# Two-block decoder: the second block's last four feed-forward groups go down in pairs, and feed-forward loops are written out

## The chip, the core and the metric

The kernel runs on one core of one Trainium2 chip. The metric is the device time of one execution in microseconds (us). On this core TensorE multiplies, ScalarE (ACT) and VectorE (DVE) prepare operands and do the elementwise work, GpSimd (POOL) does little here, and SyncE (SP) issues nearly all of the weight transfers. The engines run on their own and wait for each other through semaphores.

## What is computed

256 tokens of width 1024 go through two blocks of two layers each. The change touches the feed-forward parts. In the second block that is:

```python
def _swiglu(x, w_gate, w_up, w_down):
    h = jax.nn.silu(jnp.einsum('bsd,df->bsf', x, w_gate)) * jnp.einsum('bsd,df->bsf', x, w_up)
    return jnp.einsum('bsf,fd->bsd', h, w_down)
...
    for l in range(DEPTH):
        mix = _hybrid_mixer(x, rel_bias, w_in[l], b_in[l], w_attn_proj[l], w_ret_proj[l], w_out[l])
        x = _layer_norm(ALPHA * x + mix, ln1_g[l], ln1_b[l])
        ffn = _swiglu(x, w_ffn_gate[l], w_ffn_up[l], w_ffn_down[l])
        x = _layer_norm(ALPHA * x + ffn, ln2_g[l], ln2_b[l])
```

Here the hidden width is 2816 and all values are float32. The first block's feed-forward has a hidden width of 4096, a squared ReLU in place of the gated SiLU, and 512 hidden columns at a time.

## The kernel before

**Float32 products out of three passes.** A weight is split into a rounded part and the rest, `hi` and `lo`, and so is an activation. A product is hi x hi, plus hi x lo of the activation, plus lo of the weight x hi. The weights come in *units* of up to 4 x 128 rows by 512 columns (1 MB). Each unit is brought by SP into one of four slots (`raw`), copied by ACT into `whi` (function `hi`, L1157) and subtracted by DVE into `wlo` (function `lo`, L1600). `whi` and `wlo` have two places each, so ACT may split unit c once TensorE has used unit c - 2. SP may fill a slot once DVE has split the unit that was in it, four units back. TensorE's function `unit` (L639) waits for `hi`, does 4 matmuls for each block of 128 rows (two row tiles, two activation parts), waits for `lo` and does 2 more. A full unit is 24 matmuls of 128x512, a *half-size* unit of 2 x 128 rows is 12.

**The second block's feed-forward.** The hidden width is worked in FJ = 11 groups of 256 columns. A group needs two full units, gate and up side by side (`chunk`, 48 matmuls into PSUM pair 0). Then ACT applies SiLU and DVE multiplies (`inner2`), both on `H2`. TensorE turns the result round with 4 transposes (`inner_turn2`), ACT copies it into `MH` (`turn_hi`) and DVE subtracts into `ML` (`turn_lo`). The way down is two half-size units (`down2`, 24 matmuls into PSUM pairs 1 and 2). TensorE's order is software-pipelined: gate and up of group j + 1, down of group j, transposes of group j + 1. So the 24 matmuls of the way down cover SiLU and product. Groups 2 to 10 of gate and up are one loop, `Fori(0, FJ - 2)`, on TensorE, ACT and DVE, whose waits add 4 x i to a semaphore's value. SP's loop over the groups is already written out. The first block has a loop of 6 turns of the same kind.

**The end of a layer.** The last group's way down is done by `last_columns` (L683): the first row tile (m = 0) for both column halves, then the second (m = 1). After m = 0 `s_half` is raised, and DVE may start on the residual and the layer norm of row tile 0 (`residual`, `row_spread`, `row_norm`). Between the `hi` and the `lo` matmuls of the very last half, TensorE transposes the normalised row tile 0 for what follows (`turn_ahead`). After the last `lo` matmuls DVE does the second half of row tile 1 and its norm. In DVE's order the last group's work is followed by `lo_first` twice (the next layer's first two units, which have buffers of their own), and only then by the residual. ACT has `hi_first` twice at the same place. In the last layer there is no next layer, so these two are missing, but the transposes of row tile 0 are still made.

Of the kernel before, what the change touches and what calls it, by code (L numbers as in the profile page):

```python
# [31 lines left out]
P = 128  # L32
# [5 lines left out]
COLS = 512  # L38
UK = 4
UNIT = UK * COLS  # L40
RAW = 4
# [34 lines left out]


U_OUT, U_MLP, U_PLE0, U_DN7, U_PLE1, UNITS1 = 14, 18, 48, 49, 51, 56
V_RET, V_GATE, V_AP, V_RP, V_OUT, V_FFN, UNITS2 = 14, 30, 46, 48, 56, 60, 104
# [39 lines left out]
FIRSTS = (0, U_MLP, U_PLE1 + 1), (0, V_FFN)  # L119

# [74 lines left out]
def program(nc, a, out):  # L195
# [3 lines left out]
    with ExitStack() as ctx:  # L199
# [123 lines left out]
        s_raw = [Tally(sem(f"s_raw{n}"), (UNITS1 // RAW, UNITS2 // RAW + more), step=16)  # L323
                 for n, more in enumerate((1, 1, FJ - 1, FJ - 1))]
# [99 lines left out]
        def _(sp):  # L424
# [74 lines left out]
            for L in range(DEPTH):  # L499
# [54 lines left out]
                for k in range(2):  # L554
                    gate_up(0, V_FFN + k, k, (V_FFN + k) % RAW)
                for i in range(FJ - 1):
                    for k in range(2):
                        gate_up(i + 1, 4 * i + V_FFN + 2 + k, k, (V_FFN + 2 + k) % RAW)
                    for n in range(2):
                        src = down[bass.ds(L, 1)][:, bass.ds(i * 256, 256), n * COLS:(n + 1) * COLS].rearrange(  # L560
                            "l (k p) n -> p (l k) n", p=P)
                        unit(1, L, 4 * i + V_FFN + 4 + n, src, 2, COLS, (V_FFN + 4 + n) % RAW)
                for n in range(2):
                    unit(1, L, V_FFN + 42 + n, rows(down, L, (FJ - 1) * 256, 2, n * COLS, COLS), 2, COLS,
                         (V_FFN + 42 + n) % RAW)
# [12 lines left out]
        def landed(blk, L, i, c):  # L578

            o, slot = i + c // RAW, c % RAW  # L580
            k = o + 1
            if blk and c >= V_FFN:
                if slot < 2:
                    k = o + 2
                elif c >= UNITS2 - 2:
                    k = o + FJ
                else:
                    k = o * 2 - (2 * (V_FFN // RAW) - 17)
            return s_raw[slot].at(blk, L, k)

        def size(blk, c):
# [7 lines left out]
            small_unit = c >= UNITS2 - 2 or (c >= V_FFN + 4 and c % RAW < 2)  # L599
            return 2 * COLS if small_unit else UNIT  # L600

# [36 lines left out]
        def _(pe):  # L638
# [220 lines left out]
            for L in range(DEPTH):  # L859
# [138 lines left out]
            for L in range(DEPTH):  # L998
# [132 lines left out]
                def inner_turn2(i, j):  # L1131
                    pe.wait_ge(s_h.sem, s_h.at(1, L, i + j + 1))
                    turn(1, L, i, T2_FFN + 2 * j, H2, 2, per=1)

                def down2(i, c, first, t):
                    pe.wait_ge(s_tfree.sem, s_tfree.at(1, L, 2 * i + t))
                    for n in range(2):
                        unit(1, L, i, c + n, MH, ML, 0, 2, COLS, bank_pair(1 + n), first, False)

                first_chunk(1, L, V_FFN, T2_FX, 1, 2)  # L1140
                second_chunk(1, L, V_FFN + 2, lambda: inner_turn2(0, 0))
                down2(0, V_FFN + 4, True, T2_FFN + 2)
                inner_turn2(0, 1)
# [9 lines left out]
        def _(act):  # L1153
# [100 lines left out]
            for L in range(DEPTH):  # L1254
# [104 lines left out]
                with act.Fori(0, 6) as i:  # L1359
# [45 lines left out]
            for L in range(DEPTH):  # L1405
# [57 lines left out]
                def inner2(i, j, used, bank=0):  # L1463

                    act.wait_ge(s_used.sem, s_used.at(1, L, 4 * i + used))
                    act_(H2, pair(bank)[:, :, 0:256], ACT.Silu).then_inc(s_act.sem, 1)

                hi(1, L, 0, V_FFN + 2)
                inner2(0, 0, V_FFN + 2, 2)
                hi(1, L, 0, V_FFN + 3)  # L1470
                turn_hi(1, L, 0, T2_FFN, 2, MH, per=1)
                with act.Fori(0, FJ - 2) as i:
                    his(1, L, i, V_FFN + 4, V_FFN + 5)
                    inner2(i, 1, V_FFN + 4)
                    his(1, L, i, V_FFN + 6, V_FFN + 7)
                    turn_hi(1, L, i, T2_FFN + 2, 2, MH, per=1)
                e = 4 * (FJ - 2)
                his(1, L, 0, V_FFN + 4 + e, V_FFN + 5 + e)
                inner2(0, FJ - 1, V_FFN + 4 + e)
                his(1, L, 0, V_FFN + 6 + e, V_FFN + 7 + e)  # L1480
                turn_hi(1, L, 0, T2_FFN + 2 * (FJ - 1), 2, MH, per=1)
# [115 lines left out]
        def _(dve):  # L1597
# [208 lines left out]
            for L in range(DEPTH):  # L1806
# [154 lines left out]
                with dve.Fori(0, 6) as i:  # L1961
# [44 lines left out]
            for L in range(DEPTH):  # L2006
# [186 lines left out]
                def inner2(i, j, bank=0):  # L2193
                    dve.wait_ge(s_act.sem, s_act.at(1, L, i + j + 1))
                    tt(H2, H2, pair(bank)[:, :, 256:512], ALU.mult).then_inc(s_h.sem, 1)

                lo(1, L, 0, V_FFN + 2)
                inner2(0, 0, 2)
                lo(1, L, 0, V_FFN + 3)
                turn_lo(1, L, 0, T2_FFN, 2, MH, ML, per=1)  # L2200
                with dve.Fori(0, FJ - 2) as i:
                    los(1, L, i, V_FFN + 4, V_FFN + 5)
                    inner2(i, 1)
# [41 lines left out]
```

## Time and profile before

| | |
|---|---|
| time, median of 3 runs | 1979.17 us (1978.88 to 1979.22) |
| the profiled execution: its own time | 1976.11 us |
| its span, first to last instruction | 1974.3 us |
| busy: PE, PEld, DVE, ACT, POOL | 96%, 79%, 60%, 45%, 4% |
| the chain that ended last | PE 85%, DVE 7%, ACT 3% |
| mean granted TensorE clock | 0.979 |
| read from HBM | 333 MB, 172 GB/s over the span |

PE is TensorE's matmuls, PEld its weight loads. A matmul's shown duration (about 0.39 us) overlaps the next one's, so the spacing of starts tells the pace. The granted clock has two levels, 1.00 (2.4 GHz) and 0.50 (1.2 GHz). The chain is followed back from the last instruction to what released each one. The second block's feed-forward parts lie at 1179 to 1376 us (layer 0) and at 1783 us to the end (layer 1), the first block's loops at about 215 to 350 us and 605 to 740 us.

### The profile page before, as it was taken

The numbers are of one execution on the slowest core, as the hardware profiler recorded it, in microseconds if no ns is written. First come the engines' busy times: TensorE is split into PE (matmuls) and PEld (weight loads), VectorE is DVE, ScalarE is ACT, GpSimd is POOL, SyncE is SP. The second block draws the span as 40 slices with busy tenths as digits, with TensorE's granted clock in tenths as the row PEclk, the third lists the DMA queues.
The fourth block names the chain that finished last, engine by engine and source line by source line (L and its number), as shares of the span: only waits on it lengthen the run. The fifth ranks groups of instructions, "written<-read, shape, count | busy, mean of one in ns | idle before, by whom it ended". The sixth has DMA issues, their size and how long they took to land.

```text
span 1974.3 us, 23117 instructions
## 1 busy us (share of the span) xinstructions
PE 1897.8 (96%) x9135; PEld 1562.0 (79%) x9135; DVE 1175.4 (60%) x1368; ACT 886.3 (45%) x1071; POOL 83.3 (4%) x100
## 2 busy tenths in 40 slices
PE   7988999999899999999999999998999999999997
PEld 5877888877778888888877778887888877778885
DVE  5775554657765547456566575446556566574555
ACT  5544444555454445344345434443344355444442
POOL 6300000021100000000000000000000000000000
PEclk9988999999799999999999999999999999999998
DMA  8423555544656555654455754557563455645552
GB/s 256 142 65 113 173 189 180 196 157 135 90 173 193 189 173 208 210 189 151 144 170 175 238 174 147 183 183 242 180 222 114 152 184 189 220 156 177 185 187 89
DMA packets 194385, 340.17 MB, mean 172 GB/s; under 512 B 9342, under 2 KB 59422, under 8 KB 194304
## 3 DMA queue, kind: packets, MB, share of 16 engines
q1 hardware_dynamic: 189072, 327.76, 49.8%
q0 software_dynamic: 5232, 11.29, 3.1%
q8 instruction: 55, 0.90, 0.2%
q14 instruction: 26, 0.21, 0.0%
HBM read 333.24 MB, written 5.77 MB: 172 GB/s over the span
## 4 chain that ended last, share of the span: by engine, by line
PE 85%; DVE 7%; ACT 3%; DVEq 2%; issue 2%; DMA 0%; SPq 0%; ACTq 0%
PE G L647 19%; PE G L648 18%; PE G L652 18%; PE T L700 5%; PE A L647 4%; PE A L648 4%; PE A L652 4%; PE G L662 2%; PE G L663 2%; PE G L668 2%; DVE wlo L1605 1%; PE T L749 1%; PE A L662 1%; ACT whi L1155 1%; PE A L759 1%
## 5 line engine op out<-in xcount | busy, mean ns | idle before, releaser
L1605 DVE TENSOR_TENSOR wlo<-raw,whi 128x2048 fp32r<-128x2048 f32 (+3 forms) x300 | 630.0, 2102 | 570.6 <-ACT whi L1155 570.4
L1155 ACT ACTIVATE whi<-raw 128x2048 fp32r<-128x2048 f32 (+3 forms) x300 | 527.1, 1759 | 588.1 <-PE G L652 513.1
L647 PE MATMUL G<-whi,XH 128*128 128x512 f32 (+1 forms) x1408 | 560.1, 398 | 7.6 <-DVE XL L1619 6.3
L648 PE MATMUL G<-whi,XL 128*128 128x512 f32 (+1 forms) x1408 | 549.5, 390 | 0.0
L652 PE MATMUL G<-wlo,XH 128*128 128x512 f32 (+1 forms) x1408 | 346.2, 388 | 0.0
L647 PEld LDWEIGHTS G<-whi,XH 128*128 128x128 f32 x1408 | 266.1, 189 | 64.3 <-DVE XL L1619 8.0
L648 PEld LDWEIGHTS G<-whi,XL 128*128 128x128 f32 x1408 | 266.2, 189 | 53.9 <-issue 1.9
L652 PEld LDWEIGHTS G<-wlo,XH 128*128 128x128 f32 x1408 | 263.9, 188 | 53.6
L700 PE MATMUL T<-ident,arena 128*128 128x128 f32 x804 | 118.6, 288 | 23.0 <-ACT arena L1155 17.3
L700 PEld LDWEIGHTS T<-ident,arena 128*128 128x128 f32 x804 | 97.8, 148 | 42.1 <-ACT arena L1155 17.9
L1155 ACT ACTIVATE arena<-T 128x512 f32<-128x512 f32 (+2 forms) x92 | 46.1, 550 | 159.2 <-PE T L700 159.2
L647 PE MATMUL G<-whi,MH 128*128 128x512 f32 x216 | 84.4, 391 | 0.0
L648 PE MATMUL G<-whi,ML 128*128 128x512 f32 x216 | 84.0, 389 | 0.0
L647 PE MATMUL A<-whi,MH 128*128 128x512 f32 x192 | 74.7, 389 | 0.0
L648 PE MATMUL A<-whi,ML 128*128 128x512 f32 x192 | 74.7, 389 | 0.0
L647 PE MATMUL A<-whi,XH 128*128 128x512 f32 (+1 forms) x160 | 61.3, 385 | 0.0
L648 PE MATMUL A<-whi,XL 128*128 128x512 f32 (+1 forms) x160 | 59.8, 375 | 0.0
L1155 ACT ACT_TABLE_LOAD x40 | 51.3, 1283 | 13.6 <-PE T L700 8.1
L2013 DVE TENSOR_TENSOR arena<-G,swap 128x1024 f32<-128x1024 f32 (+1 forms) x36 | 43.4, 1206 | 22.7 <-PE G L652 18.9
L652 PE MATMUL G<-wlo,MH 128*128 128x512 f32 x216 | 55.1, 389 | 0.0
L1155 ACT ACTIVATE arena<-G,nm 128x128 f32<-128x128 f32 (+1 forms) x80 | 32.5, 418 | 47.0 <-DVE nm L1671 47.0
L1155 ACT ACTIVATE MH<-T 128x256 fp32r<-128x256 f32 (+1 forms) x82 | 33.3, 456 | 41.1 <-PE T L700 41.1
(237 smaller groups left out, 2240.1 us busy)
## 6 DMA issues: line engine op xcount, KB each, us to landing
raw<-in_w_in SPq DMA_DIRECT2D x112, 1024.0 KB, 7.2
raw<-in_w_mlp_up SPq DMA_DIRECT2D x32, 1024.0 KB, 5.3
raw<-in_w_mlp_down SPq DMA_DIRECT2D x32, 1024.0 KB, 4.9
raw<-in_w_ffn_gate SPq DMA_DIRECT2D x44, 512.0 KB, 3.7
raw<-in_w_ffn_up SPq DMA_DIRECT2D x44, 512.0 KB, 4.8
raw<-in_w_ffn_down SPq DMA_DIRECT2D x44, 512.0 KB, 3.7
raw<-in_w_out SPq DMA_DIRECT2D x16, 1024.0 KB, 4.9
raw<-in_w_ret_proj SPq DMA_DIRECT2D x16, 1024.0 KB, 5.0
```

The costliest lines, as they stand in the source:

```text
L647: nc.tensor.matmul(dst(m), hx[:, k0 + k, rows], hi[:, k, :], start=first and k == 0, stop=False)
L648: nc.tensor.matmul(dst(m), lx[:, k0 + k, rows], hi[:, k, :], start=False, stop=False)
L652: mm = nc.tensor.matmul(dst(m), hx[:, k0 + k, m * P:(m + 1) * P], lo[:, k, :], start=False, stop=last and k == kb - 1)
L662: nc.tensor.matmul(dst(m), hx[:, k0 + k, rows], hi[:, k, :], start=first and k == 0, stop=False)
L663: nc.tensor.matmul(dst(m), lx[:, k0 + k, rows], hi[:, k, :], start=False, stop=False)
L668: mm = nc.tensor.matmul(dst(m), hx[:, k0 + k, rows], lo[:, k, :], start=False, stop=last and k == kb - 1)
L700: tr = nc.tensor.transpose(T[:, t % 2, n * P:(n + 1) * P], src, ident[:])
L749: mm = nc.tensor.matmul(heads_out(q)[:, h * HD:(h + 1) * HD], PT2[m][:, h, kt, g * P:(g + 1) * P], ZV[:, kt, (g * HG + 2 * x + h) * HD:][: ...
L759: mm = nc.tensor.matmul(A[:, q % 2, u * HD:(u + 1) * HD], PT[:, q % 2, kt, u * P:(u + 1) * P], Z[:, kt, col:col + HD], start=kt == 0, stop ...
L1155: return nc.scalar.activation(out_, in_, func, **kw)
L1605: tt(lo_, raw[:, slot, 0:n], hi.bitcast(F32), ALU.subtract).then_inc(part_sem(blk, c, s_lo, s_lo1), 1)
L2013: tt(dst, pair(bank)[:, :, 0:cols], BIN[:, c % 2, 0:cols].unsqueeze(1).to_broadcast([P, TILES, cols]), ALU.add).then_inc(s_evac.sem, 1)
```

## The change

The first seven groups (FS = 7) go down as before. Groups 7 and 8 are laid side by side (in `YH`/`YL`, which are free by then) and go down as two full units of 512 rows, and so do groups 9 and 10 (in `MH`/`ML`, all four blocks). A layer has 100 units in place of 104. The way down that is in progress is cut into its column halves, one half between two groups: group 6's two half-size units follow gate and up of groups 7 and 8, the two full units of groups 7 and 8 follow those of groups 9 and 10, and `last_columns` does groups 9 and 10 with `kb` = 4. The number of matmuls, transposes and bytes is the same. SP, ACT and DVE get the same order of units. The three `Fori` loops of the first block and the three of the second are written out. The diff, cut to its core (SP's `gate_up` stays as it was; DVE's loops are edited as ACT's):

```diff
+FS = FJ - 4
-V_RET, V_GATE, V_AP, V_RP, V_OUT, V_FFN, UNITS2 = 14, 30, 46, 48, 56, 60, 104
+V_RET, V_GATE, V_AP, V_RP, V_OUT, V_FFN, UNITS2 = 14, 30, 46, 48, 56, 60, 100
+def ffn_unit(j):
+    return V_FFN + (4 * j - 2 if j else 0) - max(0, j - FS)
+def ffn_down(j, n):
+    if j < FS - 1:
+        return ffn_unit(j + 1) + 2 + n
+    return UNITS2 - 2 + n if j == FJ - 2 else ffn_unit((j if j < FS else j + 1) + n + 1) + 2
...
# SP
+                ffn_in(0)
+                for j in range(1, FS):
+                    ffn_in(j)
                     for n in range(2):
+                        down_in(j - 1, n, 2)
                 for n in range(2):
+                    ffn_in(FS + n)
+                    down_in(FS - 1, n, 2)
+                for n in range(2):
+                    ffn_in(FS + 2 + n)
+                    down_in(FS, n, UK)
+                for n in range(2):
+                    down_in(FS + 2, n, UK)
...
+        def inner_to(j, even, odd):
+            if j < FS:
+                return even
+            return (odd if j < FS + 2 else even)[:, 2 * ((j - FS) % 2):]
...
# TensorE
-                with pe.Fori(0, 6) as i:
+                for i in range(6):
...
+                def down2(j, n):
+                    pe.wait_ge(s_tfree.sem, s_tfree.at(1, L, T2_FFN + 2 * (j + (1 if j < FS else 2))))
+                    hx, lx = (YH, YL) if j == FS else (MH, ML)
+                    unit(1, L, 0, ffn_down(j, n), hx, lx, 0, 2 if j < FS else UK, COLS, bank_pair(1 + n), j == 0, False)
...
-                with pe.Fori(0, FJ - 2) as i:
-                    chunk(1, L, i, V_FFN + 6, 0)
-                    down2(i, V_FFN + 8, False, T2_FFN + 4)
-                    inner_turn2(i, 2)
+                for j in range(2, FS + 1):
+                    if j > 2:
+                        chunk(1, L, 0, ffn_unit(j - 1), 0)
+                    for n in range(2):
+                        down2(j - 2, n)
+                    inner_turn2(j - 1)
+                for j, n in ((FS, 0), (FS, 1), (FS + 2, 0), (FS + 2, 1)):
+                    chunk(1, L, 0, ffn_unit(j + n), 0)
+                    down2(FS - 1 if j == FS else FS, n)
+                    inner_turn2(j + n)
                 pe.wait_ge(s_tfree.sem, s_tfree.at(1, L, T2_FFN + 2 * FJ))
-                last_columns(1, L, V_FFN + 42, MH, ML, 0, 2, (1, 2), lambda: turn_ahead(1, L, TS2, 2))
+                last_columns(1, L, ffn_down(FJ - 2, 0), MH, ML, 0, UK, (1, 2), lambda: turn_ahead(1, L, TS2, 2))
...
# ACT
+                for j in range(1, FS):
+                    his(1, L, 0, ffn_down(j - 1, 0), ffn_down(j - 1, 1))
+                    inner2(j)
+                    his(1, L, 0, ffn_unit(j + 1), ffn_unit(j + 1) + 1)
+                    inner_hi(j)
+                for j in range(FS, FJ):
+                    hi(1, L, 0, ffn_unit(j) + 2)
+                    inner2(j)
+                    hi(1, L, 0, ffn_unit(j) + 3)
+                    if j < FJ - 1:
+                        hi(1, L, 0, ffn_unit(j) + 4)
+                    inner_hi(j)
+                hi(1, L, 0, UNITS2 - 1)
                 if L + 1 < DEPTH:
                     his(1, L + 1, 0, 0, 1)
```

ACT's order at the end of the second block's layer 0, before. It starts at the loop's last rows (the copies into `MH` and the branch). `arena<-G` is SiLU, `whi<-raw` the split of a unit (128x1024 half-size, 128x2048 full), `hi_first` the next layer's first units:

```order
L1155 ACTIVATE MH<-T 128x256
L1472 REGISTER_ALU
L1472 COMPARE_AND_BRANCH
L1155 ACTIVATE whi<-raw 128x1024 x2
L1155 ACTIVATE arena<-G 128x512
L1155 ACTIVATE whi<-raw 128x1024 x2
L1155 ACTIVATE MH<-T 128x256 x2
L1155 ACTIVATE hi_first<-raw 128x2048 x2
L1155 ACT_TABLE_LOAD
```

ACT at the same place after the change, from the last but one group on:

```order
L1190 ACTIVATE whi<-raw 128x2048
L1190 ACTIVATE arena<-G 128x512
L1190 ACTIVATE whi<-raw 128x2048 x2
L1190 ACTIVATE MH<-T 128x256 x2
L1190 ACTIVATE whi<-raw 128x2048
L1190 ACTIVATE arena<-G 128x512
L1190 ACTIVATE whi<-raw 128x2048
L1190 ACTIVATE MH<-T 128x256 x2
L1190 ACTIVATE whi<-raw 128x2048
L1190 ACTIVATE hi_first<-raw 128x2048 x2
L1190 ACT_TABLE_LOAD
```

In the last group two splits stood between SiLU and the copies into `MH`. Now one does, and the other, twice the size, stands behind the copies and ahead of `hi_first`.

DVE's order at that place before, from the last group's product (L2195) to the residual (L2153) and the norm's statistics (L2155):

```order
L2195 TENSOR_TENSOR arena<-arena,G 128x512
L1605 TENSOR_TENSOR wlo<-raw,whi 128x1024 x2
L1619 TENSOR_TENSOR ML<-T,MH 128x256 x2
L1605 TENSOR_TENSOR lo_first<-raw,hi_first 128x2048 x2
L2153 SCALAR_TENSOR_TENSOR X<-X,G 128x512
L2155 BN_STATS bns<-X 128x6
```

DVE there after the change:

```order
L2236 TENSOR_TENSOR arena<-arena,G 128x512
L1646 TENSOR_TENSOR wlo<-raw,whi 128x2048
L1660 TENSOR_TENSOR ML<-T,MH 128x256 x2
L1646 TENSOR_TENSOR wlo<-raw,whi 128x2048
L1646 TENSOR_TENSOR lo_first<-raw,hi_first 128x2048 x2
L2194 SCALAR_TENSOR_TENSOR X<-X,G 128x512
L2196 BN_STATS bns<-X 128x6
```

A full split has moved behind `ML`, so three full splits in a row stand ahead of layer 0's residual where two stood.

## Rows read from the trace of the kernel before

**Rows 1.** Chain in order of time, second block's loop: start us, us, what.

```profile
1245.27 0.44 PE T L700 x4
...
1254.80 1.81 PE G L652 x8
...
1262.05 0.44 PE T L700 x4
```

**Rows 2.** Chain in order of time, first block's loop.

```profile
246.33 0.87 PE T L700 x8
268.98 0.87 PE T L700 x8
```

**Rows 3.** Timeline, end of layer 0: start us, us, instruction, in brackets idle before.

```profile
1362.71 0.60 PE L700 MATMUL T<-ident,arena 128*128 128x128 f32 x4
1362.97 1.06 ACT L1155 ACTIVATE whi<-raw 128x1024 fp32r<-128x1024 f32 x1 [1.66 <-PE A L652]
1363.93 0.64 ACT L1155 ACTIVATE MH<-T 128x256 fp32r<-128x256 f32 x2
...
1365.20 0.75 DVE L1619 TENSOR_TENSOR ML<-T,MH 128x256 fp32r<-128x256 f32 x2
...
1366.01 0.78 PE L662 MATMUL G<-whi,MH 128*128 128x512 f32 x1 [2.69 <-DVE ML L1619]
1366.40 4.49 DVE L1605 TENSOR_TENSOR lo_first<-raw,hi_first 128x2048 fp32r<-128x2048 f32 x2 [0.45 <-ACT hi_first L1155]
...
1370.82 0.68 DVE L2153 SCALAR_TENSOR_TENSOR X<-X,G 128x512 f32<-128x512 f32 x1
...
1376.41 1.97 PE L700 MATMUL T<-ident,X 128*128 128x128 f32 x8 [3.50 <-DVE X L2172]
...
1379.27 0.69 DVE L2153 SCALAR_TENSOR_TENSOR X<-X,A 128x512 f32<-128x512 f32 x1 [0.29 <-PE A L668]
```

**Rows 4.** Timeline, end of layer 1 and of the kernel.

```profile
1949.98 0.60 PE L700 MATMUL T<-ident,arena 128*128 128x128 f32 x4
...
1953.27 0.80 PE L662 MATMUL G<-whi,MH 128*128 128x512 f32 x1 [2.69 <-DVE ML L1619]
...
1957.92 0.69 DVE L2153 SCALAR_TENSOR_TENSOR X<-X,G 128x512 f32<-128x512 f32 x1 [4.71 <-PE A L668]
...
1963.52 1.97 PE L700 MATMUL T<-ident,X 128*128 128x128 f32 x8 [3.45 <-DVE X L2172]
...
1966.38 0.69 DVE L2153 SCALAR_TENSOR_TENSOR X<-X,A 128x512 f32<-128x512 f32 x1 [0.89 <-PE A L668]
```

**Rows 5.** Timeline, single turns of the second block's groups in layer 0.

```profile
1200.12 0.60 PE L700 MATMUL T<-ident,arena 128*128 128x128 f32 x4
...
1200.54 0.66 ACT L1155 ACTIVATE MH<-T 128x256 fp32r<-128x256 f32 x2 [3.26 <-PE T L700]
...
1200.95 0.76 DVE L1619 TENSOR_TENSOR ML<-T,MH 128x256 fp32r<-128x256 f32 x2 [1.35 <-ACT MH L1155]
...
1207.21 0.58 ACT L1155 ACTIVATE arena<-G 128x512 f32<-128x512 f32 x1
...
1208.48 0.68 DVE L2195 TENSOR_TENSOR arena<-arena,G 128x512 f32<-128x512 f32 x1
...
1343.39 1.92 ACT L1155 ACTIVATE whi<-raw 128x2048 fp32r<-128x2048 f32 x1 [1.18 <-PE G L652]
```

**Rows 6.** Waits of PE, 560 to 1366 us: us in total, times, longest.

```profile
PE G L647 <- DVE XL L1619: 1.8, 1, 1.8
...
PE T L700 <- DVE X L2172: 1.2, 1, 1.2
...
PE T L700 <- issue: 0.9, 2, 0.7
```

**Rows 7.** Windows: us, busy (times) of PE, PEld, DVE, ACT, POOL, granted clock, DMA, GB/s.

```profile
1100.00:1150.00 50.00, 48.25 (x221) 39.80 (x221) 29.22 (x20) 20.20 (x16) 0.00 (x0) 1.00 0.57 190
...
1953.00:1955.00 2.00, 1.73 (x4) 1.45 (x5) 0.22 (x1) 0.14 (x1) 0.00 (x0) 0.54 0.00 0
```

More of the change, by code:

```diff
@@ L119, with loads, loads_in_slot @@
 FIRSTS = (0, U_MLP, U_PLE1 + 1), (0, V_FFN)
+def ffn_unit(j):
[4 more added lines that the diff above has]
+    return UNITS2 - 2 + n if j == FJ - 2 else ffn_unit((j if j < FS else j + 1) + n + 1) + 2
+def loads(c):
+    return 2 if c in [ffn_unit(j) + k for j in range(FJ) for k in range(2)] else 1
+def loads_in_slot(c):
+    return sum(loads(u) for u in range(c % RAW, c + 1, RAW))
 def first_no(blk, c):
@@ L320, in program @@
         A = psum("A", [P, 2, 512])
-        s_raw = [Tally(sem(f"s_raw{n}"), (UNITS1 // RAW, UNITS2 // RAW + more), step=16)
-                 for n, more in enumerate((1, 1, FJ - 1, FJ - 1))]
+        s_raw = [Tally(sem(f"s_raw{n}"), (UNITS1 // RAW, loads_in_slot(UNITS2 - RAW + n)), step=16) for n in range(RAW)]
         s_hi, s_lo = (Tally(sem(n), tuple(u - 2 * len(f) for u, f in zip((UNITS1, UNITS2), FIRSTS))) for n in ("s_hi", "s_lo"))
@@ L552, in gate_up, with ffn_in, down_in @@
                         sp.dma_start(dst[:, :, g, :], src).then_inc(s_raw[slot].sem, 16)
[L554 to L556 removed]
+                def ffn_in(j):
                     for k in range(2):
[L558 removed]
+                        gate_up(j, ffn_unit(j) + k, k, (ffn_unit(j) + k) % RAW)
+                def down_in(j, n, kb):
+                    u = ffn_down(j, n)
+                    unit(1, L, u, rows(down, L, j * 256, kb, n * COLS, COLS), kb, COLS, u % RAW)
+                ffn_in(0)
+                for j in range(1, FS):
+                    ffn_in(j)
                     for n in range(2):
[L560 to L562 removed]
+                        down_in(j - 1, n, 2)
                 for n in range(2):
[L564 to L565 removed]
+                    ffn_in(FS + n)
[5 more added lines that the diff above has]
+                    down_in(FS + 2, n, UK)
                 sp.wait_ge(s_x.sem, s_x.at(1, L, 1))
@@ L578, in landed @@
         def landed(blk, L, i, c):
[L580 to L589, printed above, removed]
+            slot = c % RAW
+            return s_raw[slot].at(blk, L, loads_in_slot(c) if blk else i + c // RAW + 1)
         def size(blk, c):
@@ L598, in size @@
                 return 3 * COLS
-            small_unit = c >= UNITS2 - 2 or (c >= V_FFN + 4 and c % RAW < 2)
+            small_unit = c in [ffn_down(j, n) for j in range(FS) for n in range(2)]
             return 2 * COLS if small_unit else UNIT
+        def inner_to(j, even, odd):
+            if j < FS:
+                return even
+            return (odd if j < FS + 2 else even)[:, 2 * ((j - FS) % 2):]
         def logit_set(q, x):
@@ L1358, in _ @@
                 turn_hi(0, L, 0, T_MLP, UK, MH)
-                with act.Fori(0, 6) as i:
+                for i in range(6):
                     his(0, L, i, U_MLP + 4, U_MLP + 5)
@@ L1960, in _ @@
                 turn_lo(0, L, 0, T_MLP, UK, MH, ML)
-                with dve.Fori(0, 6) as i:
+                for i in range(6):
                     los(0, L, i, U_MLP + 4, U_MLP + 5)
```

68 lines of the change are left out of this document (30 added, 38 removed).

## Prediction, made before the changed kernel had run

> **What bounds the kernel now.** I read the chain that ended last in order of time, first inside the feed-forward loops, then at a layer's end, then the timeline there. Inside the loops TensorE is alone on the chain. In the second block's loop 8 matmuls take 1.81 us, 0.2266 each [rows 1]. A group has 72 of them, 16.31 us, and 4 transposes of 0.44 together: 16.75. The transposes of two successive groups start 1262.05 - 1245.27 = 16.78 us apart [rows 1]. In the first block 96 matmuls (21.75) and 8 transposes (0.87) make 22.62, and two turns start 22.65 apart [rows 2]. So ACT, DVE, the transfers and the loops' own branches cost at most 0.03 us a turn. What makes such a turn shorter than its matmuls isn't in the change.
>
> The time that isn't matmul stands at the two layer ends. In layer 0 TensorE is idle 2.69 us for `ML` and 3.50 us for the normalised row tile 0 [rows 3], in layer 1 2.69 and 3.45 [rows 4]. Besides, the clock falls. After the 2.69 us the granted clock is 0.54 over two microseconds [rows 7], and 8 transposes take 1.97 us after the 3.45 [rows 4], where 8 take 0.87 in a loop [rows 2]. Who ends the chain differs. In layer 1 DVE was idle 4.71 us until TensorE's m = 0 half was done [rows 4]: the half bounds the norm. In layer 0 DVE went into the residual straight from 4.49 us of `lo_first` [rows 3]: DVE's splits bound it.
>
> **What the change does there.** Matmuls, transposes and bytes are as many as before. But 24 matmuls (the way down of group 9, 24 x 0.2266 = 5.44 us) leave the stretch ahead of the last group's transposes and join `last_columns`, where they lie beside DVE's norm. So the last transposes of a layer start 5.44 us earlier, and the question is how far the rest of the layer follows.
>
> *From the transposes to `last_columns`.* Before, that took 1366.01 - 1362.71 = 3.30 us in layer 0, 3.29 in layer 1 [rows 3, 4], since ACT had a unit to split (start 1362.97, 1.06 us) ahead of the copy into `MH`. That split can't start until group 9's way down has freed its place. In the new order one split stands there, and its place is free since gate and up ended, 5.44 us earlier; with SiLU it ends long before. What is left is the path of the open case: copy 0.42 after the transposes, `ML` ending at 1201.71, 1.59 after them [rows 5], and 0.06 to TensorE as in rows 3 (1365.95 to 1366.01). That is **1.65 us**.
>
> *Layer 1, the kernel's end.* Times from the last transposes:
> - before: 3.29, then 4.65 to the residual (1957.92 - 1953.27), 5.60 to the transposes of row tile 0, 2.86 to the last residual (1966.38 - 1963.52): 16.40 us [rows 4].
> - after: 1.65, then 24 matmuls for m = 0, 5.44, and 0.2 until DVE starts (a matmul is shown 0.39 long at a spacing of 0.23). Then 5.60 as before. TensorE is there before that: 44 matmuls after its start, 1.65 + 9.97 = 11.62 against 12.89, so it idles 1.3 us. The kernel has this tail once more, with four blocks, behind the second block's output projection, and there TensorE waits 1.2 us for the norm [rows 6]. In 1100 to 1150 us TensorE was idle 1.75 us, nearly all of it one wait of 1.8 [rows 6], and the granted clock stayed at 1.00 [rows 7], so I take the full clock here and ahead of `last_columns` too. The second half of row tile 0 comes 0.70 us after the first (two norm operations of 1.41 together on DVE, shown as 5.60 to the first). Then 4 transposes 0.44, 4 `lo` matmuls 0.91 (two more than before) and 0.2: 2.25. Sum 15.14.
>
> **Gain 16.40 - 15.14 + 5.44 = 6.7 us.** What follows (the last residual, the norm, the output's transfer) is the same.
>
> *Layer 0.* Before: 1370.82 - 1362.71 = 8.11 to the residual, 5.59 to the transposes, 2.86 to the last residual, 16.56 [rows 3]. After: the copies end and ACT starts the last full unit at about 0.96, DVE its split 1.95 later (ACT's 1.92 [rows 5] and a handover) at 2.9. Then come three full splits in a row, `wlo` and twice `lo_first`, at 2.25 each (4.49 for two [rows 3]), 6.75. ACT keeps ahead of them, at 1.92 each. The residual starts at 9.7; m = 0 is done at 7.3 and isn't late. Then 5.59. TensorE, done at 11.62, idles 3.7 us until 15.3, about the 3.50 of before, so I take the low clock that followed then: 8 transposes 1.97, 4 `lo` matmuls at 0.43 instead of two (12 matmuls of m = 0, mostly at the low clock, took 4.65 [rows 4]), 1.72, and 0.05. Sum 9.7 + 5.59 + 3.74 = 19.03. **Gain 16.56 - 19.03 + 5.44 = 3.0 us.** The moved split gives back 2.25 and the two extra `lo` matmuls behind the transposes 0.9.
>
> *The stages of groups 7 to 10.* With groups 7 and 8 the way down between gate/up and transposes is 12 matmuls, 2.72 us, half the cover. Under it lie 0.2, SiLU 0.58 and product 0.68 [rows 5], with handovers 1.6: 1.1 us to spare. In rows 5 the product starts 1.27 after SiLU's start only because DVE was on a split, which now stands elsewhere. Next, the following gate/up unit: ACT starts it after SiLU (0.7), ends at 2.6 (1.92 for a full unit [rows 5]), and TensorE wants it at 2.72 + 0.44 = 3.16. That is the narrowest place, 0.5 us. Behind it ACT waits for the half-size unit's place with the copies into `YH` queued, but those are wanted a group later. I cost the stages at **0**; without the cover each of the two would cost up to 2.7 us a layer. Each slot is refilled after DVE's split four units back, and these four units are now as long or longer in matmuls. SP passes the same units in the same order and the gains behind them. With three full units in four the next layer's first ones are asked for before the last transposes: 0.
>
> *The loops written out*, 30 turns. By rows 1 and 2 a turn has at most 0.03 us to give. No row shows new code at such a turn. The nearest are TensorE's waits for issue in straight code: 0.9 us in 800 us, 0.7 the longest [rows 6]. Ends: gain 0.9 us, loss 30 x 0.7 = 21. I take 0: most of the kernel is straight code of this density already, and its waits for issue add up to less than 1 us.
>
> The Trainium skill ("Runtime: NRT & Kernel Launch", Instruction fetch mechanics) has it that fetch is sequential in 16 KiB blocks and that a taken branch whose target isn't held costs a stall, which is why full unrolling is preferred. By that rule the loops written out should give something. The page gives no price for the stall, and the turns of rows 1 and 2 show none.
>
> **The sum.** 6.7 + 3.0 = 9.7 us. The profiled 1976.11 becomes 1966.4. The median of the runs stands 3.06 above it, so 1979.17 - 9.7 = **1969.5 us**.
>
> **The rivals.**
> 1. *The norm and the clock keep more of it.* If the clock still falls at `last_columns` and behind the norm in layer 1, about 8 matmuls and 8 transposes run at half speed: 8 x 0.2 + 1.1 + 4 x 0.2 = 3.5 us less. If layer 0 is held by late first units too, it loses up to 1.5 more. 1973.0 to 1974.5. For it: the clock did fall at both places. Against: both idles shrink to 1.65 less 0.6 and to 1.3, and 1.8 us didn't lower it.
> 2. *The half cover is too short.* If the next gate/up unit is late by 0.7 us in each of four stages, 2.8 us: 1972.3. The spare 0.5 us speaks against it.
> 3. *Slower: new code at each written-out turn.* TensorE's code for a turn now comes from memory instead of a loop body. If each of the 30 turns waited for it, at the 0.7 us of the longest issue wait [rows 6], it would be 21 - 9.7 = 11.3 slower, 1990.5. At 0.5 us it is 15 - 9.7 = 5.3, 1984.5, which I give as its time. It decides from 0.32 us a turn, and from 0.46 us it is slower by over 0.2%. Against: straight code has the same density elsewhere.
> 4. *The loops do give time.* At the 0.03 us of the turns it is 0.9 us, 1968.6. This is the way in which the Trainium skill's rule of above would work out here.
> 5. *The clock stays up in layer 0 as well*, because the low stretch falls elsewhere: transposes and `lo` at 2.25 instead of 3.74, 1.5 more: 1968.0.
>
> **How the numbers follow.** Forecast 0.52, rival 1 0.15, rival 2 0.10, rival 3 0.06, rival 4 0.05, rival 5 0.08, and 0.04 that the layer ends give nothing that I see (a wait on a transfer or a split in place of the norm's, about 1977 to 1980). A measurement of this kernel can tell about 0.2%, 4 us. Faster by more than that needs less than 1975.2: all of 0.52, 0.10, 0.05 and 0.08, and most of rival 1, and I put 0.87, a little under their sum of 0.90. Slower by 0.2%, most of rival 3: 0.05. The rest, 0.08, is within. The range takes in both ends of the layer ends' cost and leaves out rival 3: 1967.0 to 1974.5.
>
> **What would show it.** Right: idle ahead of `last_columns` about 1.1 us in both layers; 1.3 us and full clock ahead of the last transposes of row tile 0 in layer 1; three back-to-back full splits ahead of layer 0's residual; last transposes of a group at the same 16.8 us pace up to group 6. Wrong: waits of TensorE for `whi` or for H2's product in groups 7 and 8 (rival 2), waits for issue spread over the written-out turns (rival 3), a turn under 16.75 us or 22.62 (rival 4), a granted clock of 0.5 in layer 1's end (rival 1). If DVE isn't the engine that releases layer 0's residual, the 3.0 is mis-sized.

## The result: 1965.5 us, below the range

| | median | lowest to highest | executions |
|---|---|---|---|
| before, same comparison | 1979.03 us | 1976.94 to 1979.22 | 4 |
| changed kernel | 1965.49 us | 1961.50 to 1968.50 | 4 |

The ratio is 0.9933, with a 95% interval of 0.9916 to 0.9950: 13.5 us faster, where 9.7 was forecast and 1967.0 was the lower end of the range. The executions of the changed kernel spread over 7 us, those of before over 2.3. The profiled one is the fastest: 1961.50 us with a span of 1959.7, against 1976.11 and 1974.3.

The changed kernel's page, parts 1 and 3. The engines' work is what it was. TensorE has 9135 matmuls as before, and more code is loaded (73 packets and 1.20 MB on the instruction queue, 55 and 0.90 before):

```profile
PE 1887.1 (96%) x9135; PEld 1552.3 (79%) x9135; DVE 1172.7 (60%) x1360; ACT 884.5 (45%) x1063; POOL 82.2 (4%) x100
...
q8 instruction: 73, 1.20, 0.2%
```

**The end of layer 0**, the timeline of the changed kernel, which answers to [rows 3]:

```profile
1352.19 0.60 PE L730 MATMUL T<-ident,arena 128*128 128x128 f32 x4
1352.61 0.66 ACT L1190 ACTIVATE MH<-T 128x256 fp32r<-128x256 f32 x2 [3.26 <-PE T L730]
1353.02 0.75 DVE L1660 TENSOR_TENSOR ML<-T,MH 128x256 fp32r<-128x256 f32 x2 [1.35 <-ACT MH L1190]
1353.15 1.92 ACT L1190 ACTIVATE whi<-raw 128x2048 fp32r<-128x2048 f32 x1
1353.83 0.50 PE L692 MATMUL G<-whi,MH 128*128 128x512 f32 x1 [1.04 <-DVE ML L1660]
...
1355.10 2.29 DVE L1646 TENSOR_TENSOR wlo<-raw,whi 128x2048 fp32r<-128x2048 f32 x1 [1.32 <-ACT whi L1190]
...
1357.31 4.49 DVE L1646 TENSOR_TENSOR lo_first<-raw,hi_first 128x2048 fp32r<-128x2048 f32 x2
...
1361.71 0.68 DVE L2194 SCALAR_TENSOR_TENSOR X<-X,G 128x512 f32<-128x512 f32 x1
...
1365.27 1.42 DVE L2208 SCALAR_TENSOR_TENSOR X<-X,bna,gains 128x512 f32<-128x512 f32 x2 [0.24 <-issue]
...
1367.64 1.78 PE L730 MATMUL T<-ident,X 128*128 128x128 f32 x8 [3.54 <-DVE X L2213]
...
1371.16 0.69 DVE L2194 SCALAR_TENSOR_TENSOR X<-X,A 128x512 f32<-128x512 f32 x1 [0.97 <-PE A L698]
```

The copy into `MH` follows the transposes by 0.42 us, `last_columns` starts 1.64 after them (3.30 before), and three full splits stand in a row ahead of the residual. TensorE still waits 3.54 us for the norm. From the last transposes to the last residual it is 1371.16 - 1352.19 = 18.97 us; 19.03 was worked out. The parts are further off than the sum: 9.52 us to the residual (9.7 worked out), 5.93 from there to the transposes of row tile 0 (5.59), 3.52 from there to the last residual (3.74). The middle one has its cause in the row of L2208: DVE pauses 0.24 us for issue, that is, it waits for nothing that the profile shows. Five later kernels don't have this pause, and there the same way takes 5.59 or 5.60 us (`pairs_only`, `pairs_first_written`, `pairs_second_written`, `pairs_shift60`, `late_split`).

**The end of layer 1** in the changed kernel, which answers to [rows 4]:

```profile
1936.38 0.60 PE L730 MATMUL T<-ident,arena 128*128 128x128 f32 x4
...
1938.02 0.50 PE L692 MATMUL G<-whi,MH 128*128 128x512 f32 x1 [1.04 <-DVE ML L1660]
...
1943.87 0.69 DVE L2194 SCALAR_TENSOR_TENSOR X<-X,G 128x512 f32<-128x512 f32 x1 [2.29 <-PE A L698]
...
1949.47 1.32 PE L730 MATMUL T<-ident,X 128*128 128x128 f32 x8 [1.18 <-DVE X L2213]
...
1951.76 0.69 DVE L2194 SCALAR_TENSOR_TENSOR X<-X,A 128x512 f32<-128x512 f32 x1 [0.32 <-PE A L698]
```

15.38 us against 15.14 worked out. TensorE waits 1.18 us for the norm (1.3 expected, 3.45 before), and 8 transposes take 1.32 us against 1.97: here the clock stayed up.

**So the ends gave what the sum said**: 5.44 + 16.56 - 18.97 = 3.03 us in layer 0 (3.0) and 5.44 + 16.40 - 15.38 = 6.46 in layer 1 (6.7), 9.5 together. The spans of the two profiled executions differ by 14.6. The other 5.1 us came about outside the two layer ends. The table compares the spacing of the same TensorE instructions in the two traces, stretch by stretch, before minus after (times as in before):

| stretch | gained |
|---|---|
| start to 111 us | -1.4 us |
| 111 to 192 us, first block's attention, layer 0 | 4.7 |
| 192 to 474 us, loops of layer 0 among it | -0.4 |
| 474 to 592 us, attention, layer 1 | 2.0 |
| 592 to 1340 us, three more loops | 0.2 |

The windows of the two kernels show what differs in the attention of layer 0: the granted clock over 150 to 200 us. Changed kernel:

```profile
100.00:150.00 50.00, 41.98 (x304) 36.19 (x304) 39.10 (x91) 21.63 (x80) 4.37 (x9) 0.86 0.20 64
150.00:200.00 50.00, 44.29 (x223) 36.32 (x224) 31.85 (x60) 25.97 (x51) 0.00 (x0) 1.00 0.35 113
```

The kernel before:

```profile
100.00:150.00 50.00, 43.10 (x300) 37.54 (x297) 37.97 (x88) 22.51 (x82) 3.31 (x8) 0.83 0.19 63
150.00:200.00 50.00, 45.52 (x205) 37.41 (x204) 29.00 (x56) 22.48 (x42) 0.00 (x0) 0.86 0.32 111
```

Up to there the two kernels run the same instructions in the same order, so this part can't be the change's doing. The experiments had to say which part of the rest is.

### The profile page after: what moved, and what is told of

It reads as the page before. It is cut to its first block, busy times and chain, and to the rows that moved or that the text cites. A ratio compares the mean times of both kernels' runs of the same rounds, so it can differ in the third digit from the quotient of the medians.

```text
span 1959.7 us, 22425 instructions
## 1 busy us (share of the span) xinstructions
PE 1887.1 (96%) x9135; PEld 1552.3 (79%) x9135; DVE 1172.7 (60%) x1360; ACT 884.5 (45%) x1063; POOL 82.2 (4%) x100
## 4 chain that ended last, share of the span: by engine, by line
PE 85%; DVE 8%; ACT 3%; DVEq 3%; issue 1%; DMA 1%; SPq 0%; ACTq 0%
PE G L677 19%; PE G L678 18%; PE G L682 18%; PE T L730 5%; PE A L677 4%; PE A L678 4%; PE A L682 4%; PE G L692 2%; PE G L698 2%; PE G L693 2%; DVE wlo L1646 2%; PE T L779 1%; PE A L692 1%; ACT whi L1190 1%; PE A L698 1%
## 5 line engine op out<-in xcount | busy, mean ns | idle before, releaser
L677 PE MATMUL G<-whi,MH 128*128 128x512 f32 x192 | 75.1, 391 | 0.0
L678 PE MATMUL G<-whi,ML 128*128 128x512 f32 x192 | 74.7, 389 | 0.0
L677 PE MATMUL A<-whi,MH 128*128 128x512 f32 x168 | 65.4, 389 | 0.0
L678 PE MATMUL A<-whi,ML 128*128 128x512 f32 x168 | 65.4, 389 | 0.0
L1660 DVE TENSOR_TENSOR ML<-T,MH 128x256 fp32r<-128x256 f32 (+1 forms) x74 | 36.4, 533 | 23.4 <-ACT MH L1190 23.4
```

The source lines that it names most:

```text
L677: nc.tensor.matmul(dst(m), hx[:, k0 + k, rows], hi[:, k, :], start=first and k == 0, stop=False)
L678: nc.tensor.matmul(dst(m), lx[:, k0 + k, rows], hi[:, k, :], start=False, stop=False)
L1660: ins = tt(lx[:, b:b + k, :], src, hx[:, b:b + k, :].bitcast(F32), ALU.subtract)
```

## The experiments

Theory A: the layer ends give 9.5 us, the loops nothing, and the rest is the clock in the attention. Rival B: the written-out loops give it. The medians of one table below come from one comparison on one chip. The kernel before itself had medians of 1977.0 to 1978.3 us in the three comparisons, so medians of different tables compare to about 1 us.

### Loops alone, pairs alone

`loops_only` is the kernel before with its six loops written out:

```diff
-                with pe.Fori(0, 6) as i:
+                for i in range(6):
...
-                with pe.Fori(0, FJ - 2) as i:
+                for i in range(FJ - 2):
```

and the same on ACT and DVE.

> The kernel before with its six feed-forward loops written out and nothing else. Theory A: a loop's turn is only its matmuls, so writing it out gives nothing; what the changed kernel gained beyond the two layer ends was TensorE's clock in the first block's attention, which differs from execution to execution: within 1 us of the kernel before in the medians (1978 to 1980), turns 22.65 and 16.8 us apart. Rival B: the loops written out give the 3 to 4 us by which the changed kernel beat the sum: 1975 to 1976.

`pairs_only` is the changed kernel with loops:

```diff
-                for i in range(6):
+                with pe.Fori(0, 6) as i:
...
-                for j in range(2, FS + 1):
...
+                with pe.Fori(0, FS - 2) as i:
+                    chunk(1, L, i, V_FFN + 6, 0)
...
```

> The changed kernel with its loops rolled up again (6 turns in the first block, 5 on TensorE and 6 on ACT and DVE in the second); the pairs stay. Theory A: as the changed kernel, 9.5 us under the kernel before (1969 to 1970) where the clock in the attention is the same; from the last group's transposes to the last residual 19.0 us in layer 0 and 15.4 in layer 1. Rival B: 9.5 us under the kernel before, but 3 to 4 us over the changed kernel of this call.

> The changed kernel once more, beside the others. Theory A: executions spread over some 7 us (1961 to 1969 so far) in step with the mean granted clock, about 1 us for each 0.0005 of it, and the stretches outside the first block's attention repeat to 0.3 us. Rival C: it is 13 to 14 us under the kernel before throughout, with little spread, and the gain of the stretch ahead of the first loop is the same in every trace.

| kernel | median | lowest to highest | n | mean clock |
|---|---|---|---|---|
| before | 1978.31 us | 1974.30 to 1981.03 | 15 | 0.9784 |
| `loops_only` | 1975.97 | 1975.61 to 1978.44 | 11 | 0.9787 |
| `pairs_only` | 1969.23 | 1967.88 to 1971.41 | 5 | 0.9812 |
| `after_again` | 1967.70 | 1964.03 to 1969.38 | 5 | 0.9828 |

By the medians, the pairs alone give 9.1 us (ratio 0.9958, interval 0.9944 to 0.9971, which is 8.3 us). The loops alone give 2.3, not resolved (0.9994, 0.9985 to 1.0003, which is 1.2 us), with the pairs 1.5. A line fitted through the executions of one kernel, time over mean clock, falls by 1.4 us for each 0.001 for the changed kernel (five) and by 1.7 for before (fifteen), so much of the spread goes with the clock; the eleven of `loops_only` show no such slope (0.1). `loops_only` came out in rival B's range. The changed kernel's lead of 1.5 us over `pairs_only` lies between theory A's 0 and rival B's 3 to 4. In the traces, though, the loops aren't shorter: in `loops_only` the stretch from 592 to 1340 us, with three loops, takes 0.2 us less, and the stretch from 192 to 474 us, with one, takes 0.37 more. Nearly all of the 0.37 arises behind the loop: up to 373.9 us DVE pauses 0.45 us for issue in the layer norm, where the kernel before has no pause, and TensorE's next transposes are 0.32 late. The same pause stands at 369.0 in the changed kernel.

The expectation for `after_again` asked whether the gain of the first attention is the same in every trace (rival C). It isn't: from 111 to 192 us the three profiles of the changed kernel (the first, `after_again`, and `after_third` of the next table) gained 4.7, 2.3 and 0.0 us over before's, and outside the attention and the start they agree to 0.1. So in the first profile the 4.7 us were luck.

### Which loops?

> The changed kernel with only the second block's loops rolled up (the first block's are written out). Theory A (the loops' form is worth nothing; the executions differ by TensorE's clock in the first block's attention): stretches outside the attention as in the changed kernel within 0.4 us, and a median of 1966 to 1970, whichever way the clock falls. Rival B, that written-out loops of the first block give some 2 us: 2 us under pairs_second_written, at the same mean clock too.

> The changed kernel with only the first block's loops rolled up. Theory A: as pairs_first_written within the spread of the executions, 1966 to 1970. Rival B': if the second block's written-out loops give the 2 us, this one has them and pairs_first_written hasn't; in the trace the two second-block loops would then be shorter than the 16.8 us a turn of before.

> The changed kernel a third time, for the spread. Theory A: the executions fall on the line of the earlier ones, 1.3 to 1.5 us less for each 0.001 of mean granted clock, median 1965 to 1969, and the profile differs from the other two of this kernel only at the start and in the first block's two attention stretches. If these stretches agree with the earlier profiles to 0.3 us and the median still differs, the clock isn't the reason.

| kernel | median | lowest to highest | n |
|---|---|---|---|
| before | 1977.03 us | 1973.79 to 1981.11 | 11 |
| `pairs_first_written` | 1966.45 | 1960.41 to 1968.30 | 6 |
| `pairs_second_written` | 1969.32 | 1968.44 to 1969.42 | 5 |
| `after_third` | 1966.72 | 1964.35 to 1968.55 | 5 |

Over both tables, the two kernels with the first block's loops rolled up stand at 1969.2 and 1969.3, the three sets of executions with pairs and the first block's loops written out at 1967.7, 1966.5 and 1966.7. The second block's loops are worth nothing that can be seen here. The first block's are worth 2.6 to 2.9 us in the second table and 1.5 in the first, and theory A is wrong in that. The line that theory A expected of `after_third` fits less well too: 0.7 us for each 0.001 in its five executions, where 1.3 to 1.5 was expected.

**Where it is.** I followed the same TensorE instruction through all the traces of both forms. From 474 to 485 us (attention of layer 1, right behind layer 0's loop and the layer's other parts) they agree to 0.01 us. Then one step comes: the transposes that stand at 487.43 in before come 1.32 us earlier in `loops_only` and `pairs_first_written` and in all other kernels with the first block's loops written out (1.30 to 1.32 in seven traces), and 0.00 to 0.01 in before, `pairs_only` and `pairs_second_written`. DVE's timeline has the reason. The kernel before, index scores and the first softmax's maximum:

```profile
478.19 2.16 DVE L1838 SCALAR_TENSOR_TENSOR SCO<-arena,IW,SCO 128x256 f32<-128x256 f32 x4
480.82 2.42 DVE L1838 SCALAR_TENSOR_TENSOR SCO<-arena,IW,SCO 128x256 f32<-128x256 f32 x3 [0.47 <-issue]
483.33 1.35 DVE L1841 TENSOR_TENSOR SCO<-SCO,swap 128x256 f32<-128x256 f32 x1
```

The kernel before, GpSimd's rotation beside it:

```profile
481.36 0.73 POOL L625 TENSOR_TENSOR gains<-arena,sind 128x256 f32<-128x256 f32 x1 [10.20 <-ACT arena L1155]
482.05 0.91 POOL L626 TENSOR_TENSOR gains<-arena,sind 128x256 f32<-128x256 f32 x1
483.10 1.30 POOL L628 TENSOR_TENSOR arena<-arena,cosd 128x512 f32<-128x512 f32 x1
```

DVE in `loops_only`:

```profile
480.31 4.15 DVE L1838 SCALAR_TENSOR_TENSOR SCO<-arena,IW,SCO 128x256 f32<-128x256 f32 x7
484.56 0.78 DVE L1841 TENSOR_TENSOR SCO<-SCO,swap 128x256 f32<-128x256 f32 x1
```

Before, DVE stands still for 0.47 us for issue in the middle of seven operations of one kind. Its last ones then run beside three operations of GpSimd. From the first of the seven to the end of the last it takes 5.05 us where `loops_only` takes 4.15, of which 0.45 is the pause and the rest one more operation beside GpSimd. L1841 then takes 1.35 instead of 0.78, since it meets POOL L628. That is 1.47 us on DVE; `loops_only` starts the seven 0.12 us later, and some 1.3 are left. TensorE's waits in the two show it arriving. Before, 484 to 488 us, then `loops_only`, 484.5 to 489.6 us:

```profile
PE T L700 <- ACT arena L1155: 1.9, 1, 1.9
```

```profile
PE T L700 <- ACT arena L1155: 0.6, 1, 0.6
```

The Trainium skill ("SBUF — State Buffer", SBUF: two separate sides) says that a DVE operation with two inputs in SBUF and a GpSimd operation that reads SBUF need one port pair, which is an exclusive lock: whichever starts first holds it for its whole instruction. L1838 and L1841 have two such inputs, and the traces agree. Before, POOL L628 runs from 483.10 to 484.40 us and L1841 ends at 484.68, 0.28 us behind it. In `loops_only` L1841 starts beside a shorter operation of GpSimd:

```profile
484.14 0.92 POOL L626 TENSOR_TENSOR gains<-arena,sind 128x256 f32<-128x256 f32 x1
```

This one ends at 485.06, and L1841 at 485.34, again 0.28 us behind it. So the 0.78 us is a lengthened time as well, and the pause made L1841 miss the short operation and meet the long one.

Behind the step the low clock of 3.4 us that starts at 488.8 in before, after the longer wait, is missing at that place in the written-out form. By 493 us the lead is 2.95 us. By 592 us later low stretches have taken most of it back: 0.65 to 0.83 us are left in five of these traces, 2.0 and 3.4 in two.

### Is it the loops or the place of the code?

Theory D: DVE's pause is tied to a place in its code, and the loops merely moved it. Then empty instructions must do the same.

```diff
+                if L == 0:
+                    for _ in range(20):
+                        dve.drain()
                 with dve.Fori(0, 6) as i:
```

> The kernel with pairs and rolled loops (pairs_only), with 20 empty instructions (drains) on DVE ahead of the first block's loop of layer 0, where DVE has slack: the code behind them moves by 20 places. Theory D: in all kernels with the first block's loops rolled up DVE pauses 0.46 us for issue in the middle of the index scores at about 481 us and then collides with GpSimd, which costs 1.3 us and a low-clock stretch; written-out loops only moved that pause. Then the pause leaves that place here too, the transposes at 487 us come 1.3 us earlier relative to what stands before, the low clock from 489 us is missing, and the median falls from 1969.3 to 1966 to 1967.5. If the written-out form itself gives the time (rival B), nothing moves: 1969.3.

> The same with 60 empty instructions. Theory D: the pause stands at a third place; as long as that isn't in the scores just ahead of a wait, 1966 to 1967.5 as well (the drains themselves cost at most 1 us). Rival B: 1969.3 or up to 1 us more.

> The kernel before with the same 20 empty instructions and nothing else. Theory D: 1975 to 1976.5 beside 1977 to 1978.3 for the kernel before, as the kernel before with written-out loops had (1975.97), with the pause gone from 481 us. Rival B: no difference from the kernel before.

| kernel | median | lowest to highest | n | the 1.32 us step |
|---|---|---|---|---|
| before | 1977.27 us | 1975.00 to 1981.47 | 15 | no |
| `pairs_shift20` | 1967.48 | 1964.41 to 1968.40 | 5 | no |
| `pairs_shift60` | 1966.35 | 1965.49 to 1967.78 | 5 | yes |
| `before_shift20` | 1980.33 | 1976.20 to 1982.49 | 11 | no |

The pause moved with the code. `pairs_shift20`, some 20 instructions ahead of where it stood:

```profile
473.84 0.29 DVE L1898 MATCH_REPLACE8 SCO<-m,SCO 128x128 f32<-128x128 f32 x1 [0.33 <-issue]
...
477.08 4.71 DVE L1886 SCALAR_TENSOR_TENSOR SCO<-arena,IW,SCO 128x256 f32<-128x256 f32 x7
481.89 1.35 DVE L1889 TENSOR_TENSOR SCO<-SCO,swap 128x256 f32<-128x256 f32 x1
```

`pairs_shift60`:

```profile
466.60 0.29 DVE L1896 MAX8 m<-SCO 128x8 f32<-128x128 f32 x1 [0.46 <-issue]
...
478.70 4.15 DVE L1886 SCALAR_TENSOR_TENSOR SCO<-arena,IW,SCO 128x256 f32<-128x256 f32 x7
482.94 0.78 DVE L1889 TENSOR_TENSOR SCO<-SCO,swap 128x256 f32<-128x256 f32 x1
```

Counted over all of DVE's instructions in the trace, drains and the turns of the loops included, the pause stands ahead of the same one, number 660 from 0, in all six traces with the first block's loops rolled up, with 0, 20 or 60 empty ones ahead of it. The kernels without loops have pauses at numbers 447, 703, 1343 and 1471 (the fourth shows in `loops_only` and `pool_split`, the third in the changed kernel), which are 256, 640 and 128 apart. Before has four, at 660 and 788 and, behind a loop, at 1129 and 1257. All these distances in straight code are multiples of 128. So writing the loops out took the pause off the index scores and put others at 369.0 and 1365.27 us of the changed kernel, where they cost 0.3 us each.

With 60 the loops are rolled up, and the kernel has the step (1.34 us), the short L1889 and a median of 1966.35, that of the written-out form. For the step that rules out rival B: the loops' form isn't needed. With 20 my expectation failed. The pause left the scores, but at 473.8 it is still in DVE's unbroken run of work ahead of them, so DVE reaches them as late as before and meets GpSimd all the same (4.71 for seven, 1.35). `before_shift20` came out 3 us slower than the kernel before, ratio 1.001 (1.000 to 1.002), where 1 to 2 less was expected. It too lacks the step, which takes away the reason for a gain. Its profile, 6.0 us longer than before's, is 2.1 us behind by 192 us, ahead of the edit. It has 3.4 us of low clock at 1535 us that before's hasn't (1.6 us), and at the end of layer 0 its low clock comes in one stretch of 6.8 us behind the norm, where before has 3.4 there and 3.4 at `last_columns` (1.0 us). Why they fall so is open. Likewise `pairs_shift20` has no step and still is 1.8 us under the other two kernels with pairs and no step; its profile gained 2.4 us in layer 0's attention by clock alone. So the step is shown by the traces, and what the medians owe to it less firmly. Counted from 474 us, the eight traces with the step (that of `pairs_shift60` too) stand 0.5 to 3.4 us ahead of before at 592 us, the four others without it 0.0 to 2.7 behind. On average that is 2.3 us between the two kinds, which fits the 1.5 to 2.9 of the medians, but it rests on one trace of each set, and the medians of the two kernels with 20 empty instructions don't follow it.

### What holds layer 0's norm

> The changed kernel with one edit: DVE splits the second of the next layer's first units after the first residual of row tile 1, not ahead of row tile 0's norm. If three full splits in a row are what holds layer 0's norm (theory A), the residual starts 2.25 us earlier, TensorE's wait for the norm falls from 3.5 to about 1.3 us, the clock stays at 1.00 there, and layer 0 gains 2 to 3 us; layer 1 is unchanged. If TensorE's half or ACT held it, nothing moves.

```diff
                 if L + 1 < DEPTH:
-                    los(1, L + 1, 0, 0, 1)
+                    lo(1, L + 1, 0, 0)
...
                     row_lo(1, L + 1, 0, 0, 0)
+                    lo(1, L + 1, 0, 1)
```

`late_split`, the end of layer 0:

```profile
1354.69 0.60 PE L730 MATMUL T<-ident,arena 128*128 128x128 f32 x4
...
1362.19 0.69 DVE L2194 SCALAR_TENSOR_TENSOR X<-X,G 128x512 f32<-128x512 f32 x1
...
1367.79 1.32 PE L730 MATMUL T<-ident,X 128*128 128x128 f32 x8 [1.19 <-DVE X L2213]
...
1370.27 2.28 DVE L1646 TENSOR_TENSOR lo_first<-raw,hi_first 128x2048 fp32r<-128x2048 f32 x1
1372.47 0.68 DVE L2194 SCALAR_TENSOR_TENSOR X<-X,A 128x512 f32<-128x512 f32 x1
```

The wait is 1.19 us and the clock stays up, as expected, and the transposes of row tile 0 come 13.10 us after the last group's, not 15.45. But the moved split now stands ahead of the last residual, which starts at 17.78 instead of 18.97. The gain is 1.2 us, not 2 to 3, and 0.34 of it is the pause at L2208, which this kernel hasn't. The median was 1966.31 beside 1967.70 for the changed kernel, 1.4 less, within the spread of both. It is the lower of the two by trace and by median, and 12 us under the kernel before (0.9943, 0.9930 to 0.9957).

> The changed kernel with the second of the next layer's first units split by GpSimd instead of DVE (only between layers 0 and 1 of the second block). If DVE's third full split is what holds layer 0's norm, the residual starts at 7.5 us after the last transposes, the transposes of row tile 0 at 13.1 and the last residual at 15.4, as in layer 1: 3.5 us less than the changed kernel, 1964 in the median. If GpSimd takes longer than 12 us for it, or slows DVE beside it, half of that or nothing.

```diff
+                if L + 1 < DEPTH:
+                    pool.wait_ge(*part_done(1, L + 1, 0, 1, s_hi, s_hi1))
+                    pool.wait_ge(*part_done(1, L + 1, 0, 0, s_lo, s_lo1))
+                    hi1, lo1 = weights(1, 1, UNIT)
+                    tt(lo1, raw[:, 1, 0:UNIT], hi1.bitcast(F32), ALU.subtract).then_inc(s_lo1.sem, 1)
```

`pool_split`, GpSimd's split and DVE's norm beside it:

```profile
1359.24 0.60 PE L730 MATMUL T<-ident,arena 128*128 128x128 f32 x4
...
1366.80 4.60 POOL L1639 TENSOR_TENSOR lo_first<-raw,hi_first 128x2048 fp32r<-128x2048 f32 x1 [476.06 <-DVE lo_first L1651]
...
1369.97 2.64 DVE L2213 SCALAR_TENSOR_TENSOR X<-X,bna,gains 128x512 f32<-128x512 f32 x2
...
1373.57 1.32 PE L730 MATMUL T<-ident,X 128*128 128x128 f32 x8 [2.42 <-DVE X L2218]
...
1376.04 0.68 DVE L2199 SCALAR_TENSOR_TENSOR X<-X,A 128x512 f32<-128x512 f32 x1
```

The residual started 7.5 us after the last transposes, as expected, but then the two norm operations L2213 took 2.64 us in place of 1.41. The first of them alone took 1.97 instead of 0.75: it started while GpSimd worked and ended 0.55 us behind GpSimd's operation. The transposes came at 14.33 and the last residual at 16.80, 2.2 us before the changed kernel's, not 3.5. The median, 1967.02 beside 1966.72, doesn't show it; one execution of six was at 1957.37 with a mean clock of 0.989. By trace it gains, by median nothing is shown.

## Why the prediction was wrong

The time was 1.5 us under the range's lower end and 4.0 under the forecast.

- **Matmuls alone bound the loops: right.** In all the traces a turn keeps its length; the changed kernel's transposes are at 243.06, 265.72 and 288.37 us in the first block.
- **From the transposes to `last_columns`, 1.65 us: right**, 1.64 in both layers. The clock stayed up there, which rival 1 doubted.
- **Layer 1, 6.7 us: right**, 6.46. Two places differ: m = 0 to the residual took 5.85 in place of 5.64, and behind the norm 2.29 instead of 2.25.
- **Layer 0, 3.0 us: the sum is right**, 3.03, and `late_split` shows that DVE's three splits were its bound. That it fits to 0.06 is luck: its parts were off by -0.18, +0.34 (the pause at L2208) and -0.22 us.
- **The two ends together, 9.7 us: right.** From 1309 us on, ahead of the first pair, the eight profiles of kernels with the pairs and this layer end gained 9.4 to 9.9 us over before's.
- **Groups 7 to 10, cost 0: right.** Transposes of groups 6, 7, 8, 9 and 10 of the changed kernel stand at 1290.58, 1304.67, 1318.74, 1335.56 and 1352.35 us in the chain. With half the cover a stage takes 14.08 us, and its 60 matmuls (13.60) and transposes (0.44) make 14.04. Rival 2 is out.
- **What the low clock costs the transposes: misread.** The 1.97 us of a timeline row was set against the 0.87 of the chain. At the full clock the same row shows 1.32 (layer 1 above).
- **The loops written out, "I take 0": this step failed.** It was costed by turns alone, from gain 0.9 to loss 21 us, and the waits for issue that it rested on, less than 1 us, were TensorE's alone. DVE's, in the same profile of before, were four of 0.4 to 0.5 us, two of them:

```profile
DVE SCO L1838 <- issue: 0.5, 1, 0.5
DVE arena L1697 <- issue: 0.5, 1, 0.5
```

  What the edit did was to move the code behind the first block's loops, and with it the first of these pauses, off a place where it cost 1.3 us and a low-clock stretch. Kernels with pairs and the first-block loops rolled up are at 1969.2 and 1969.3 us, those with them written out at 1966.45 to 1967.7: 1.5 to 2.9 us.
- **Nothing said about the rest of the kernel's spread: a second failed step.** The sum was set on a median as if executions repeated to 0.3 us. They don't: 14 executions of the changed kernel go from 1961.5 to 1969.4, median 1966.8, 45 of before from 1973.8 to 1981.5, median 1977.3. From these the gain is 10.5 us. The first four of each were 1.3 us low for the changed kernel and 1.8 high for before. In the profiled pair 4.7 us came from the clock in layer 0's attention, ahead of any edit.

So of the 4.0 us, 1.3 are the luck of the four executions, and the rest is about what the first block's loops give in the medians. That the pairs with rolled loops came out at the forecast of 1969.5 is luck too: against the kernel before in the same comparison they gained 9.1 and 7.7 us, and the 1979.17 on which the sum was set is 1.9 above the median of all 45.

Of the rivals, 4 had the sign (1968.6), but for a reason that the traces refute: no turn got shorter. Rival 3 was wrong: new code at 30 turns didn't slow TensorE. Rival 5 was out too: 3.4 us of low clock followed the wait of 3.54 us in layer 0.

What is settled is where the pause stood and what it cost there, by eight traces with the step and five without. That the pause is a wait for the next block of code is an inference: it is shown as issue, and its places keep distances of 128 instructions or multiples of it. Of the two instruction queues of the profile one loads 8 KB at a time (q14, 0.21 MB in 26 loads) and one 16 KB (q8, 0.90 MB in 55); which of them serves DVE no view says. Settled isn't how the low-clock stretches fall in the rest of the attention, which gave or took up to 3 us a trace, and with it how much of the medians' 1.5 to 2.9 us is the pause; the traces speak for some 2.3.

## What to carry to other kernels

When a tail is bound by a chain on another engine, move independent matmuls behind the point where that chain starts: here 24 matmuls a layer gave 9.5 us at two layer ends, and the sum from single rows of the timeline was right to 0.2 us. Look at whose queue the moved preparation lands in, since the split that moved with them gave back 2.25 us in layer 0.

Rewriting a loop shifts all code behind it, so read the waits for issue of every engine and not of the busiest alone, and compare stretches that weren't edited before crediting a gain to the edit. A few empty instructions in a variant tell a place effect from a real one, by its trace; its median alone didn't tell here. Where the clock moves on its own, four executions can miss the gain by 3 us.

## What the runs showed of the hardware

- Pauses of 0.24 to 0.47 us on DVE for issue in runs of small operations, whose place moves with the number of instructions ahead: at 480.8 us in before, with pairs and 20 empty instructions at 473.8, with 60 at 466.6. They stand at DVE's instruction 660 in six traces, and their distances in straight code are multiples of 128.
- DVE operations with two operands from SBUF beside GpSimd ones: in all 13 traces those of 256 columns that start while GpSimd works, at 478 to 486 us, end 0.28 or 0.29 us behind GpSimd's operation, so that the same one took 0.78 or 1.35 us. In `pool_split` two of 512 columns that take 1.41 took 2.64. GpSimd needed 4.60 us for a 128x2048 subtraction that DVE does in 2.25.
- A 0.5 us event can cost 3 us on the way: the longer wait was followed by a granted clock of 0.5 for 3.4 us.
- The same wait isn't always followed by the low clock. TensorE's 2.69 us ahead of `last_columns` in layer 0 was in before, and 2.7 in `before_shift20` wasn't. Its idles of 1.04 and 1.18 us at the new layer ends and of 2.42 in `pool_split` weren't either.
- The same instructions gave 30.7 us of low clock in layer 0's attention in before's profile and 13.7 in the changed kernel's.
